# Turning the retention's keys and values and the attention's softmaxed weights with VectorE block transposes and trips through DRAM in a hybrid encoder trunk

## What is computed

```python
# retention, 4 heads of 64; here in chunks of 64 tokens
scores = einsum('bcqhd,bcshd->bchqs', q, k) * decay_mask
o_inner = einsum('bchqs,bcshe->bcqhe', scores, v)
kv = einsum('bcshd,hs,bcshe->bchde', k, k_decay, v)   # state update
# windowed attention, 4 query heads on 2 key heads, 16 meta keys + 2 chunks of 64
pr = sink_softmax(einsum('bcqkgd,bcskd->bckgqs', qr, kb), sink, valid)
orr = einsum('bckgqs,bcskd->bcqkgd', pr, vb)
# both layers: proj = h @ w_in[i]; mixers; h = norm(a*h + mix @ w_out)
#              h = norm(a*h + silu-gated mlp(h))
```

## Time and profile before

| | us |
|---|---|
| median of 3 runs | 3055.97 |
| lowest and highest | 3054.97, 3060.37 |
| profiled execution | 3056.32 |
| its span in the trace | 3054.4 |

### The profile page before, as it was taken

The page is one execution under the profiler, slowest core; times in us unless marked ns, Lnnn a source line. Parts: engine busy times, 40 slices in busy tenths (PEclk is TensorE's granted clock), DMA queues, the critical chain, the costliest instruction groups (busy, mean ns, idle before and its releaser), DMA issues.

```text
span 3054.4 us, 64343 instructions
## 1 busy us (share of the span) xinstructions
PE 3011.8 (99%) x27180; PEld 2759.9 (90%) x27180; DVE 1529.4 (50%) x3672; ACT 939.6 (31%) x2381; POOL 216.8 (7%) x319
## 2 busy tenths in 40 slices
PE   8999999999999999999999999999999999999998
PEld 7788778889898899989989899999999999999998
DVE  4345552355633455336554366544566255663562
ACT  3324440134421343124341144303343043421320
POOL 0111010011101110010010101000000000000000
PEclk9999999999999999999999999999999999999999
DMA  7577477788978989888797898986768857787887
GB/s 256 170 205 213 118 208 218 220 237 283 311 236 263 280 273 320 242 259 272 238 313 210 264 276 261 295 284 196 260 205 268 290 178 249 210 267 253 301 302 248
DMA packets 227116, 760.19 MB, mean 249 GB/s; under 512 B 25088, under 2 KB 44672, under 8 KB 226576
## 3 DMA queue, kind: packets, MB, share of 16 engines
q1 hardware_dynamic: 189328, 620.80, 61.6%
q0 software_dynamic: 37504, 135.28, 18.0%
HBM read 744.33 MB, written 136.31 MB: 288 GB/s over the span
## 4 chain that ended last, share of the span: by engine, by line
PE 92%; DMA 3%; DVE 3%; ACT 2%; issue 0%; SPq 0%; ACTq 0%; DVEq 0%
PE psum L1853 29%; PE psum L1306 27%; PE psum L1876 10%; PE psum L1912 8%; PE psum L1443 7%; DMA slots<-in_weights 2%; PE psum L1300 1%; PE psum L1322 1%; PE psum L1621 1%; PE psum L1646 1%; DMA slots<-wsum 1%; PE psum L1633 1%; PE psum L1572 1%; PE psum L1694 1%; PE psum L1803 1%
## 5 line engine op out<-in xcount | busy, mean ns | idle before, releaser
L1306 PE MATMUL psum<-hT,slots 128*128 128x256 f32 (+1 forms) x2880 | 658.9, 387 | 2.8 <-ACT hT L874 2.1
L1306 PEld LDWEIGHTS psum<-hT,slots 128*128 128x128 f32 x2880 | 541.6, 190 | 97.0 <-issue 5.5
L1853 PE MATMUL psum<-tsum,slots 128*128 128x128 f32 (+1 forms) x4928 | 608.0, 277 | 11.6 <-ACT raw L1223 4.9
L1853 PEld LDWEIGHTS psum<-tsum,slots 128*128 128x128 f32 x4928 | 573.1, 191 | 28.6 <-issue 20.2
L1853 PE MATMUL psum<-hT,slots 128*128 128x128 f32 (+1 forms) x3696 | 453.7, 276 | 6.9 <-DMA slots<-in_weights 3.9
L1853 PEld LDWEIGHTS psum<-hT,slots 128*128 128x128 f32 x3696 | 432.6, 192 | 10.1 <-DMA slots<-in_weights 4.9
L1876 PE MATMUL psum<-gT,slots 128*128 128x256 f32 (+1 forms) x1408 | 309.9, 383 | 0.0
L1876 PEld LDWEIGHTS psum<-gT,slots 128*128 128x128 f32 x1408 | 267.1, 190 | 40.9
L1306 PE MATMUL psum<-mixT,slots 128*128 128x256 f32 (+2 forms) x1024 | 226.4, 381 | 1.1 <-DVE hT L2030 1.1
L1306 PEld LDWEIGHTS psum<-mixT,slots 128*128 128x128 f32 x1024 | 194.3, 190 | 29.7 <-issue 1.5
L2030 DVE SCALAR_TENSOR_TENSOR hT<-hT,psum 128x256 f32<-128x256 f32 (+2 forms) x96 | 40.5, 423 | 348.3 <-PE psum L1876 249.7
(11 more groups left out here) (326 smaller groups left out, 3526.6 us busy)
## 6 DMA issues: line engine op xcount, KB each, us to landing
slots<-in_weights SPq DMA_DIRECT2D x667, 512.0 KB, 4.6
slots<-wsum SPq DMA_DIRECT2D x308, 512.0 KB, 4.5
wsum<-in_weights POOLq DMA_DIRECT2D x132, 512.0 KB, 6.7
slots<-wsumi SPq DMA_DIRECT2D x64, 512.0 KB, 4.4
slots<-wsumd SPq DMA_DIRECT2D x64, 512.0 KB, 4.5
wsum<-wsum POOLq DMA_DIRECT2D x44, 512.0 KB, 7.9
wsumi<-in_weights POOLq DMA_DIRECT2D x24, 512.0 KB, 7.5
wsumd<-in_weights POOLq DMA_DIRECT2D x24, 512.0 KB, 9.3
```

What stands on the lines that cost most here:

```text
L1306: ins = mm(psum[:, i % 2, :n], lhsT, rhs, start=k == 0, stop=k == len(pairs) - 1)
L1853: ins = mm(dst[:, e * n:(e + 1) * n], w[:, (4 * e + k) * P:(4 * e + k + 1) * P], moving[s][k], start=s in (0, 1, 5) and e == 0 and k == 0, ...
```

## The change

**Keys and values.** For u > 0 the two tiles with j > 0 (14 tiles) are no longer turned by PE. Once for a chunk, VectorE turns the 32x32 blocks of `rows` (rk0, rk1, rv0, rv1; two tiles) into `kvcut`, 128x1024. SP writes that to `kvdram` (512 KB) and reads it back in four DMAs of 128 KB, with the blocks exchanged, into `kvturned`, which shares its memory with the scores of the attention. VectorE makes `rKt` in two operations and ScalarE `rVt` in two, from SBUF.

**Weights of the softmax.** For u > 1 and j > 0 (12 tiles) PE's eight transposes and ScalarE's copies into `PT` go. VectorE turns the blocks in two operations (512 and 384 columns) into `PC`, SP writes them to `pdram` (512 KB) after the block that stands four behind the block of the tile's second step, and reads them back in four DMAs three blocks later. The tile has six steps, and the product with the values stands at the sixth, where it waits for `cut_in`.

**Semaphores.** Both use `cut` (VectorE has turned), `cut_out` (the write has landed) and `cut_in` (the read has). The scratch for POOL's DMA descriptors goes from 2048 to 1024, and POOL clears the padding once.

```diff
@@ SP, after the wait for block i-5
+                    if name0[:2] == "us" and AT[u0, name0] in turns:
+                        what, k = turns[AT[u0, name0]]
+                        (weights_to_dram if what == "put" else weights_by_keys)(k)
+                    if u0 and name0 in ("cb1", "is3_2"):
+                        keys_to_dram(u0)
+                    if u0 and name0 in ("sq0", "is3_5"):
+                        keys_by_tokens(u0)
@@ SP
+            def keys_to_dram(u):
+                sp.wait_ge(S["cut"], keys_cut(u) + 1)
+                if keys_cut(u):
+                    sp.wait_ge(S["cut_in"], 64 * keys_cut(u))
+                sp.dma_start(kvdram, kvcut).then_inc(S["cut_out"], 16)
+            def keys_by_tokens(u):
+                sp.wait_ge(S["cut_out"], 16 * (keys_cut(u) + 1))
...
+                for b in range(4):
...
+                    sp.dma_start(kvturned[here]..., source[b]).then_inc(S["cut_in"], 16)
+            def weights_to_dram(nth):
+                sp.wait_ge(S["cut"], nth + 1)
+                sp.wait_ge(S["cut_in"], 64 * nth)
+                sp.dma_start(pdram, sc[:, 0:1024]).then_inc(S["cut_out"], 16)
+            def weights_by_keys(nth):
+                sp.wait_ge(S["cut_out"], 16 * (nth + 1))
...
+                for q in range(4):
+                    sp.dma_start(PB[...]..., source[q]).then_inc(S["cut_in"], 16)
@@ ACT, retention
+                    if keys_by_blocks(u, j):
+                        a.wait_ge(S["cut_in"], 64 * (keys_cut(u) + 1))
+                        for ct in range(2):
+                            ins = act(rVt[...], kvturned[:, (j - 1) % 2, :, 2 + ct], ACT.Copy)
@@ PE, retention
+                    if not keys_by_blocks(u, j):
+                        for ct in range(2):
+                            transpose(bank(BX)[:n_, ct * P:(ct + 1) * P], row(f"rk{ct}", n_, off), P)
+                            ins = transpose(bank(BX)[...], row(f"rv{ct}", n_, off), P)
@@ PE, attention, behind three yields
+                    if weights_by_blocks(u, j):
+                        yield
+                        yield
+                        pe.wait_ge(S["cut_in"], 64 * (weights_cut(u, nth) + 1))
...
+                        ins.then_inc(S["a_oT"], 1)
+                        yield
+                        continue
@@ DVE, input part
+                    if u and name == "cx1":
+                        cut_keys(u)
...
                     rest(sums)
+                    cut_keys(u)
                     keep_window()
+            def cut_keys(u):
...
+                read_out(u, "is1_6" if u in IN_FAST else "rv1")
+                v.wait_ge(S["r_rope"], 4 * u + 4)
+                v.wait_ge(S["a_mix"], tiles_before(u))
...
+                v.transpose(kvcut..., rows[:, r:r + 4, ...]...).then_inc(S["cut"], 1)
@@ DVE, attention
+                    if weights_by_blocks(u, j):
+                        after(step(ins))
+                        for m in range(2):
+                            ins = v.transpose(PC[:, 0:4 - m, m]..., PR[...]...)
+                        ins.then_inc(S["cut"], 1)
@@ program
-    nc = bacc.Bacc(..., dynamic_dma_scratch_size=2048)
+    nc = bacc.Bacc(..., dynamic_dma_scratch_size=1024)
```

More of the change, by code:

```diff
@@ L116 @@
 DN_BLOCKS = 3
+ALL_TILES = [(u, j) for u in range(NU) for j, _, _ in tiles_of(u)]
 DN_SLOTS = 8 * DN_BLOCKS
@@ L124, with keys_by_blocks, weights_by_blocks, tiles_where @@
 SWA_PART = ["sq0", "sq1", "sk", "sv"]
+def keys_by_blocks(u, j):
+    return u > 0 and j > 0
+def weights_by_blocks(u, j):
+    return u > 1 and j > 0
+def tiles_where(test, nth):
+    return sum(test(*tile) for tile in ALL_TILES[:nth])
+def keys_cut(u):
+    return u - 1 + tiles_where(weights_by_blocks, tiles_before(u))
+def weights_cut(u, nth):
+    return u + tiles_where(weights_by_blocks, nth)
+def tiles_not(test, nth):
+    return nth - tiles_where(test, nth)
 def input_part(u):
@@ L202, with lane_block, weight_turns @@
 AT = {key: i for i, key in enumerate(BLOCKS)}
+PUT_AFTER, GET_AFTER = 4, 7
 assert len(AT) == len(BLOCKS)
+def lane_block(u, step):
+    return AT[u - 1, f"us{step // 3}_{2 * (step % 3) + 1}"]
+def weight_turns():
+    out = {}
+    for nth, (u, j) in enumerate(ALL_TILES):
+        if weights_by_blocks(u, j):
+            i, nt, k = [t for t, _, _ in tiles_of(u)].index(j), len(tiles_of(u)), weights_cut(u, nth)
+            start = 3 * nt + 3 + (5 if nt == 3 else 0) + 6 * (i - (nt == 3))
+            out[lane_block(u, start + 1) + PUT_AFTER] = ("put", k)
+            out[lane_block(u, start + 1) + GET_AFTER] = ("get", k)
+    return out
 def sum_points(l):
@@ L515, in build @@
             "r_tr", "r_kc", "r_vc", "r_sc", "r_sm", "r_state", "r_o", "r_oc", "r_ssq", "r_sd", "r_mix",
-            "a_kept", "a_window", "a_vt", "a_vtc", "a_sc", "a_scm", "a_max", "a_exp", "a_es", "a_pn", "a_pt", "a_ptc",
+            "a_kept", "a_window", "a_vt", "a_vtc", "a_sc", "a_scm", "a_max", "a_exp", "a_es", "a_pn", "cut", "cut_out", "cut_in", "a_pt", "a_ptc",
             "a_oT", "a_mix",
@@ L695, in _ @@
             g.memset(PCp, 1.0).then_inc(S["init"], 1)
+            g.memset(sc[:, 28 * BLOCK:1024], 0.0).then_inc(S["init"], 1)
             g.wait_ge(S["in_con"], 16)
@@ L1731, in side @@
                         pe.wait_ge(S["r_oc"], nth)
[L1732 to L1735, removed]
+                    if not keys_by_blocks(u, j):
+                        for ct in range(2):
+                            transpose(bank(BX)[:n_, ct * P:(ct + 1) * P], row(f"rk{ct}", n_, off), P)
+                            ins = transpose(bank(BX)[:n_, 256 + ct * P:256 + (ct + 1) * P], row(f"rv{ct}", n_, off), P)
+                        ins.then_inc(S["r_tr"], 1)
                     yield
@@ L2340, in product_out @@
                 return psum[:, SMALL_BANK[name], :chunk_of(u)[1]]
+            def cut_keys(u):
+                stored = 2 * max(u - NCH - 2, 0)
+                for b in range(2 if stored else 0):
+                    v.wait_ge(s_out[b], 64 * (stored // 2))
+                read_out(u, "is1_6" if u in IN_FAST else "rv1")
+                v.wait_ge(S["r_rope"], 4 * u + 4)
+                v.wait_ge(S["a_mix"], tiles_before(u))
+                first = META if u % NCH == 0 else 0
+                r = ROW["rk0"]
+                v.transpose(kvcut.rearrange("p (c r s) -> p c r s", c=8, r=4),
+                            rows[:, r:r + 4, 2 + first:2 + first + 2 * P].rearrange("p r (c s) -> p c r s", c=8)
+                            ).then_inc(S["cut"], 1)
             def rotations(u):
```

70 lines of the change are left out of this document (58 added, 12 removed).

## The result

The changed kernel is slower: 3161.6 us median of 4 runs (3156.5 to 3165.9) against 3057.95 of the kernel before (3055.0 to 3060.4), a ratio of 1.0339 (95% interval 1.0317 to 1.0361). That is 104 us. The forecast was 3099, range 3067 to 3130: the direction was right, the size was far too small.

What follows compares the result with a forecast made beforehand. The prediction took TensorE (PE), busy for 99% of the span, to bound the kernel. Its terms summed as 3056.3 - 18.1 + 26 + 5.5 + 5.5 + 16 + 5 + 3 = 3099 us, range 3067 to 3130.

Steps and rivals of the forecast that it cites:

- What comes off PE: Transposes of twelve attention tiles (11.2 us) and 14 retention tiles (6.9 us) leave PE, all on the path: -18.1 us.
- SP's wait at `sk`: Input part of chunks 4 to 7: `sk` load held behind the keys' write, which waits for VectorE; 6.5 each, +26 us.
- (a): Faster rival: SP's list has enough lead in the input parts, no wait reaches PE; 3038 to 3041 us, chance 0.08.
- (c): Rival: the second product's reads stall, but SP's wait in the input parts doesn't reach PE; 3067 us, chance 0.05.
- The clock: PE at half clock after stalls over 2 us, 1.37 each: +5.5 for four input parts, +5 for four second-product stalls.
- The keys in chunks 1 to 3: Reads wait for the write's landing ahead of `us0_1`'s load: 3.5 in chunk 3, 2 in chunk 2, 0 in chunk 1; +5.5 us.
- The second product: Attention's product with the values waits 3.2 for its reads at six of eight tiles in u = 2 to 5: +19 us.
- its neighbours: PE's existing load waits in some stretches around the second product are moved away by its new waits: -3 us.
- VectorE: Added VectorE work delays the RWKV state product at second tiles, half a microsecond in six: +3 us (0 to 13).
- (d): DMA saturation rival: 6.5 us at each of eight second-product tiles, smaller POOL scratch working the same way; 3135 us, chance 0.13.
- (b): Rival: input-part waits as forecast, but the second product's reads are covered in busy stretches too; 3078 us, chance 0.17.
- (e): Rival: the transposes' time doesn't come off PE, which fills it with load waits; 3099 + 18 at most, chance 0.02.

Runs made afterwards that it cites:

- e11: Changed kernel with trips only for keys of chunks 4 to 7 and softmax weights of 6 and 7, keys' transpose before token sums, weights' reads one block earlier: 3044.7 us.
- e7: Changed kernel without any of the 19 DRAM trips, consumers waiting only for VectorE's block transposes: 3044.4 us against 3057.2 for the kernel before.
- e3: Changed kernel with VectorE's block transpose of the keys moved ahead of the four token sums in chunks 4 to 7: 3126.7 us against 3054.8 for the kernel before.
- e5: Changed kernel with reads taking same-size weight blocks, so SP needn't wait for the write's landing; consumers wait for both: 3142.8 us against 3057.2 for the kernel before.
- e4: Kernel before with only the scratch for POOL's DMA descriptors changed, 1024 in place of 2048: 3055.2 us against 3054.8.
- e10: Changed kernel without POOL's sums of the weights, plain blocks in their place: 3081.0 us; the kernel before, also without them, took 3043.3.

## Why the prediction was wrong in size

- **What comes off PE, -18.1.** Right within about 2 us: in e11 PE's busy time is 9.4 lower, of which 7.6 had been expected from the transposes and 1.7 are clock; in e7, with all of them gone, it is 12.6 lower with 3.4 more lost to the clock, so 16.0.
- **SP's wait at `sk`, +26.** Right in mechanism and size: 6.84, 6.43, 6.53 and 6.62, together 26.4, and they vanish when the block transpose moves ahead of the sums (e3). In chunk 7 the load of `sk` left 0.37 us behind the write and was there 4.91 later, where 0.65 and 4.6 had been added: the two small errors cancel. Rivals (a) and (c), in which this wait doesn't reach PE, fall.
- **The clock, +5.5 and +5.** This step failed, 10.5 against 38. Its price of 1.37 us for each stall came from one short stretch of the earlier trace rows, and it counted eight stalls. The trace has sixteen half-clock stretches with work of PE behind the start. The four at `sk` lost 2.0 to 2.8 each, 9.0 in all (in chunk 7 the two blocks themselves 2.07, 9.14 against 7.07). The three behind the keys' waits in chunks 1 to 3 lost 7.5, for which nothing had been added. The others, nearly all in chunks 2 to 5, lost 21.6 in place of 5: one behind two stalls close together, at 834 and 843, 5.3 alone.
- **The keys in chunks 1 to 3, +5.5.** Measured 5.88, 3.29 and 3.91 of idle, 13.1. In chunks 2 and 3 the mechanism was right (the forecast had 2 and 3.5, at `us0_1`). Chunk 1 had been given nothing, without a reason; there PE waited at a block of the input part. POOL's sums are near it: their transfers start at 22.3 us in the kernel before and the last are issued at 1953.5, so they lie beside chunks 0 to 5, and not only beside chunks 1 to 4. The timeline of SP and PE in chunk 1 and the DMA view from 274 to 286:

```profile
284.80 2.62 SPq L696 DMA_DIRECT2D SC<-kvdram  x4
...
295.62 6.70 PE L1412 MATMUL psum<-hT,slots 128*128 128x272 f32 x15 [5.88 <-DMA slots<-in_weights]
...
wsum<-in_weights POOLq DMA_DIRECT2D x2, 512.0 KB, 6.9
kvdram<-prpt SPq DMA_DIRECT2D x1, 512.0 KB, 8.8
```

The write landed in 8.8 us, and the reads left SP at 284.80 only then, with the loads behind them.
- **The second product, +19, and its neighbours, -3.** This step failed too. Measured 33.0 of idle at the product, and at blocks, nearly all in chunks 2 to 5, not 3 less but 10 more. All eight tiles of chunks 2 to 5 waited, 0.60 to 7.51 us, where six had been given 3.2; in chunks 6 and 7, where none had been forecast, two waited for 1.90 and 0.55. Two things failed. The reads of a train were priced by the landings of an older train (2.4 and 6.8); measured, from first issue to last landing, they took 7.4 to 13.1 us in busy stretches and 6.0 to 7.8 in quiet ones, not 9.4 and 5.0. And the sentence that SP's wait for the landing of the write "is the same delay as above" in busy stretches left the write out of the sum: there it took 5.5 to 13.7 us to land, and the reads left with its landing in place of on time. e5 shows that this wait of SP is not the cause in itself, since with the reads sent off ahead of the landing the product still waited for 34.5 us. What has to be priced is the whole trip, 19.3 us in the mean beside POOL's transfers against 12.1 to 13.1 in chunks 6 and 7. The room of 6.2 us was read rightly: at the first tile of chunk 7 the product began to wait at 2754.5, 6.3 after the reads had left at 2748.2.
- **VectorE, +3.** Not contradicted: e7 shows 1.0 of idle, and 5 as the most that its time allows.
- **The rivals.** (d), saturation, 3135, had the right direction: without POOL's traffic the loss is 37.7 us. Its 52 us of idle around the second product were more than the 43 measured; it fell short of the result because it left the clock as it was and the keys in chunks 1 to 3 too. The range, which ended at 3130, left out even (d)'s own number. Its side remark on the scratch falls (e4). (b) falls, since the product waited in every busy stretch, and (e), since the transposes' time did come off.
- **Added up, idle:** 26 + 5.5 + 16 + 3 = 50.5 forecast, 86.3 measured; clock 10.5 forecast, 38 measured. The forecast missed by 62.6 us against the median and by 66.9 against the profiled execution. Of that, 27.5 are clock, 27 idle time at the second product and its neighbours, and 7.6 at the keys. All went one way: the last two, and the clock behind them, hang on one quantity, the landings beside POOL's transfers, with which some 66 us of the loss go (e10).

What stays open: in e10 the reads of second tiles take longer than those of first tiles, 7.6 to 8.5 us in five of six against 5.9 to 6.7. SP's loads shortly before them may be the cause, but no run took that alone. Open is also what makes the landings late beside POOL's transfers, the turns of the queues or the memory.

## What to carry to other kernels

A trip through DRAM that replaces a fraction of a microsecond of the bounding engine pays only where its whole latency (write, landing, train of reads) is covered in that stretch's own traffic; price it from landings in the same stretch, with other queues at work, not from the median. A DMA that waits in an in-order load queue for another engine needs that engine's result ahead of every long wait of that engine: one line moved gave back 32 us. And a stall of TensorE is to be priced with the half-clock work behind it, which came to almost half of the idle time here (38 of 86 us).

## What the hardware showed that was not expected

- In the changed kernel a 512 KB write to DRAM landed in 3.0 to 4.4 us in quiet stretches and in 5.5 to 13.7 with POOL's queue at work; in one such stretch, 2019 to 2034, loads of the same size took 10.9 and 11.5 us in the median.
- Issuing the reads sooner under that load hardly made them land sooner: the eight trips took 19.0 us in the mean in e5 and 19.3 in the changed kernel, from the issue of the write to the last landing. Without POOL's sums the same eight took 12.1 to 13.8 (e10).
- A wait of 1.90 us, at 2414.91 in the changed kernel, was already followed by work at half clock (from 2418.0), though PE had been busy at full clock before it (1.00 granted from 2405 to 2414).
